# Which experts a mixture-of-experts stage starts with, how its columns are filled, and its first and last step taken out of the loop

## The chip, the cores and the metric

The kernel runs on one core of one Trainium2 chip. The metric is device time in microseconds (us), read as the median of a few runs; lower is better. Before the change the median of three runs was 944.57 us (943.24 to 945.4).

## The reference, cut to what matters

The program is one denoising step of a two-layer backbone: layer 0 mixes tokens with an RWKV-7 and a convolution branch, layer 1 with differential attention. Each layer ends in a mixture of experts (MoE), and only that part is changed. Two streams of 128 tokens of width 1024 pass through it, a prompt and a sample:

```python
def hier_moe(h, rg_w, rg_b, re_w, re_b, w_gate, w_up, w_down):
    g_idx = argmax(h @ rg_w + rg_b)                  # one of 4 groups
    e_in = (h @ re_w + re_b) of the chosen group     # 8 experts in it
    top_v, top_i = lax.top_k(e_in, 2)                # two experts for each token
    gates = one_hot(g_idx * 8 + top_i) * g_p * softmax(top_v)
    hid = silu(h @ w_gate[e]) * (h @ w_up[e])        # 1024 -> 256
    out = (hid * gates) @ w_down[e]                  # 256 -> 1024
```

With 256 tokens and two picks each there are 512 picks. The weights of one expert are 1024 x 512 (gate and up) and 256 x 1024 (down) in float32: 3 MiB.

How the picks fall for this input, by evaluating the reference's router (picks of prompt and sample together; experts that nobody picked are left out):

| layer | expert: picks |
|---|---|
| 0 | 0: 91, 1: 33, 2: 48, 3: 47, 4: 51, 5: 4, 6: 24, 7: 134, 8: 1, 9: 1, 24: 18, 25: 16, 26: 5, 27: 2, 28: 13, 29: 3, 30: 18, 31: 3 |
| 1 | 8: 67, 9: 45, 10: 157, 11: 98, 12: 15, 13: 3, 14: 69, 15: 4, 16: 2, 17: 2, 18: 3, 19: 6, 20: 5, 24: 2, 25: 4, 26: 2, 27: 4, 28: 10, 30: 8, 31: 6 |

## The kernel before

The MoE of a layer runs in steps. One step handles 128 slots: four *columns* (`NC = 4`) of 32 slots (`CH = 32`), and each column belongs to one expert. An expert with n picks needs n/32 chunks, rounded up: 28 chunks and so 7 steps in layer 0, 32 chunks and 8 steps in layer 1. Each column has one buffer for one expert's weights (`EW[:, c]`), of three parts: gate and up for the first four tiles of the width (`gu0`, 1 MiB), for the other four (`gu1`, 1 MiB), and `down` (1 MiB). A part is reloaded as soon as TensorE (PE) is through with it in the step before, and only if the column's expert changes (the flags `M_LOAD` in `meta`). SyncE (SP) issues these loads in the order gu0, gu1, down of step i, then gu0 of step i+1, and it waits before each part for PE.

One step on PE: the gate and up products (line 1282, first half on gu0, second on gu1), the *gather* of the next step's tokens by a product with a 0/1 selection matrix (L1247), two pairs of transposes (L1295, L1298), the *scatter* of the last step's result into the sums (L1258), the down product (L1310). ScalarE (ACT) and VectorE (DVE) copy results out of PSUM and form the hidden values between them; DVE also builds the selection and gate matrices of the next step.

What stands ahead of the loop. Experts of step 0 are chosen from the prompt's counts alone, while the sample's stream is still being normalised: `first_keys` and `first_ranks` rank the experts by these counts, and the four least picked (above zero) are the first step's, so that their 12 MiB of weights can be on the way. When both streams' counts are there, DVE works out the rest: chunks of the remaining experts in order of their number, cut into four equal runs, one for each column; the expert and the reload flag of each step and column go to `meta` as integers, and `sig(..., "meta")` releases SP, ACT, PE and DVE, which all read the number of steps from it. Only then does any of them enter its loop.

`warm(n)` issues n dummy products on PE where it would idle. GpSimd (POOL) waits for the second step's down product and then loads the gate rows and norm parameters that the stage after needs (L765, L756; 2 MiB).

Of the kernel before, what the change touches and what calls it, by code (L numbers as in the profile page):

```python
# [15 lines left out]
ALU = mybir.AluOpType  # L16
# [46 lines left out]
NCST = C_G4 + 64  # L63


def constants():
# [22 lines left out]
    c[:, C_M8:C_M8 + 8] = np.arange(8) - 1000.0  # L89
    return c  # L90
# [97 lines left out]
def build(nc, a, o):  # L188
# [41 lines left out]
    small = view(region(320), 320)  # L230
# [19 lines left out]
    BK2 = Banks(ps, [6], S("filled_side"), {"dve": S("drained_side")})  # L250
# [184 lines left out]
    def plan_first(l):  # L435
        for h2 in range(2):
            BK.add(("xT", f"e{l}", 0, h2), "act" if h2 == 0 else "dve")
        if l == 0:
            BK.add(("mix", 0, 1, 0), "dve")
        BK.add(("lg", l, 0), "dve")  # L440
        for kind in ("first", "ranked", "early"):
            BK.add((kind, l), "dve")
        if l == 0:
            BK.add(("mix", 0, 1, 1), "dve")

    def plan_moe(l):
# [9 lines left out]
        for kind in ("base", "eid"):  # L456
            BK2.add((kind, l), "dve")

# [149 lines left out]
    R_EID, R_F, R_RF, R_F4 = 952, 1004, 1036, 1068  # L608
    R_FLAG, R_D = R_ZERO, R_ZERO + 64
# [24 lines left out]
    def _(sp):  # L634
# [26 lines left out]
        for l in range(2):  # L661
# [17 lines left out]
            steps = sp.value_load(meta[0:1, 0, 0:1], min_val=MINS, max_val=MAXT)  # L679
            with sp.Fori(1, steps) as it:  # L680
# [9 lines left out]
                sp.wait_ge(S(f"down{l}"), it * 2 + 2)  # L690
# [21 lines left out]
    def _(pool):  # L712
# [63 lines left out]
        for l in range(2):  # L776
# [4 lines left out]
            pool.wait_ge(S(f"down{l}"), 6)  # L781
# [20 lines left out]
    def _(pe):  # L802
# [376 lines left out]
        def first_rows(l):  # L1179
# [3 lines left out]
            pe.matmul(bank[0:1, 0:NC], cst[0:32, C_COL:C_COL + 1], rt_[0:32, R_F4:R_F4 + NC], start=True, stop=True)  # L1183
            pe.matmul(bank[:, 32:64], rt_[0:32, R_NB:R_NB + P], ident[0:32, 0:32], start=True, stop=True)
            pe.matmul(bank[:, 64:96], rt_[0:32, R_ZERO:R_ZERO + P], ident[0:32, 0:32], start=True, stop=True)\
                .then_inc(filled, 1)

# [10 lines left out]
        first_rows(0)  # L1198
        project_out(0, 1, 1, range(7, KT))


        def moe(l):
# [5 lines left out]
            filled_side = S("filled_side")  # L1208
            rows(l, 0)
# [20 lines left out]
            side_free("base")  # L1230
            pe.wait_ge(S("nchunks"), l + 1)
            bank, nb = side("base"), rt_[0:32, R_NB:R_NB + P]
            pe.matmul(bank[:, 0:32], nb, SU[0:32, 0:32], start=True, stop=True)
            pe.matmul(bank[:, 32:33], nb, ones[0:32, 0:1], start=True, stop=True)
            pe.matmul(bank[0:32, 64:65], UI[0:32, 0:32], nb[:, 0:1], start=True, stop=True).then_inc(filled_side, 1)
# [6 lines left out]
            def gather(n, tiles=range(KT)):  # L1242

                pe.wait_ge(S(f"selected{l}"), n + 1)
                for k in tiles:
                    for s in range(NS):
                        mm = pe.matmul(ps[:, 4 + k // 4, (k % 4) * P:(k % 4 + 1) * P], hb[:, s, k * P:(k + 1) * P],  # L1247
                                       sel[:, s, :], start=(s == 0), stop=(s == 1))
                    if k % 4 == 3:
                        mm.then_inc(S(f"gathered{l}"), 1)  # L1250

            def scatter(n):

                pe.wait_ge(S(f"y_read{l}"), n + 2)
                pe.wait_ge(S(f"y_read_dve{l}"), n + 2)
                for s in range(NS):
                    for half in range(2):
                        mm = pe.matmul(ps[:, 2 * s + half, :], tG[:, s * P:(s + 1) * P],  # L1258
                                       ysb[:, half * 512:(half + 1) * 512], start=False, stop=False,
                                       skip_group_check=True)  # L1260
                return mm

            warm(6)
            gather(0, range(4))
            side_free("eid")
            pe.wait_ge(S("ended"), l + 1)
            pe.matmul(side("eid")[0:1, 0:NC * MAXS], ones[0:32, 0:1], rt_[0:32, R_CMP:R_CMP + NC * MAXS],
                      start=True, stop=True).then_inc(filled_side, 1)

            gather(0, range(4, KT))  # L1270
            pe.wait_ge(S("cleared"), 4 * l + 4)
            BK2.wait_drained(pe, ("eid", l))
            pe.wait_ge(S(f"meta{l}"), 1)
            steps = pe.value_load(meta[0:1, 0, 0:1], min_val=MINS, max_val=MAXT)
            with pe.Fori(0, steps) as n:
                pe.wait_ge(S(f"xg_act{l}"), n + 1)
                pe.wait_ge(S(f"xg_dve{l}"), n + 1)
                for h in range(2):
                    pe.wait_ge(S(f"gu{h}_loaded{l}"), n * 64 + 64)
                    for k in range(4 * h, 4 * h + 4):  # L1280
                        for c in range(NC):
                            mm = pe.matmul(ps[32 * c:32 * c + 32, 6, :], xg[:, k, 32 * c:32 * c + 32],  # L1282
                                           EW[:, c, k * 512:(k + 1) * 512],
                                           start=(k == 0), stop=(k == KT - 1), skip_group_check=True)
# [1331 lines left out]
```

## Time and profile before

| | us |
|---|---|
| median of 3 runs | 944.57 |
| the profiled execution | 940.24 |
| its span | 938.4 |
| PE busy in it | 845.4 |
| DVE busy in it | 493.0 |

The MoE of layer 0 is the stretch from about 422 to 568 us of the span (7 steps), that of layer 1 from about 758 to 920 us (8 steps). The remaining 2 us of the execution's time lie around the span. In the timeline a row of PE is a run of equal instructions; the trace counts two matmul records for each float32 product. "[5.57 <-DMA ...]" behind a row is the idle time of that engine just before it and what ended it.

### The profile page before, as it was taken

Reading aid. Unit: us, or ns where it says so; the run is one execution under the profiler, and the core shown is the slowest. Engines: PE = TensorE matmul, PEld = TensorE weight load, DVE = VectorE, ACT = ScalarE, POOL = GpSimd, SP = SyncE. Lnnn points to the kernel's source line nnn. Section 1 sums busy time; section 2 is a strip of 40 time slices with the busy share of each in tenths; the row PEclk is TensorE's granted clock in tenths of the full one; section 3 lists DMA queues with packets and bytes.
Section 4 is the critical chain, followed back from the end, with each engine's and each line's share of the span. In section 5 each row is a group of like instructions: output and inputs, shape, how many; then the busy total and the mean of one; then the engine's idle time right before and its main releaser. Section 6 shows DMA issues by size and latency. Waiting matters only on the chain. (4 is left out here: it accounts for less than half of the span.)

```text
span 938.4 us, 14579 instructions
## 1 busy us (share of the span) xinstructions
PE 845.4 (90%) x5328; PEld 516.2 (55%) x5328; DVE 493.0 (53%) x1287; ACT 192.3 (20%) x538; POOL 41.9 (4%) x62
## 2 busy tenths in 40 slices
PE   3899989999999989989799978999879887999893
PEld 0687865777677675573345435444555752444351
DVE  1244589898864684675224426011375771432356
ACT  0125631222211211121111101110562210111110
POOL 1000140000000000000000001000000000000000
PEclk9999999999999999999899989999999998999997
DMA  9941269565454410099989785544100699989961
GB/s 366 411 181 68 90 253 415 194 264 184 153 213 181 186 38 34 20 409 421 418 322 413 282 373 203 216 179 159 66 1 1 262 422 421 373 344 404 420 262 45
DMA packets 29071, 226.85 MB, mean 242 GB/s; under 512 B 4105, under 2 KB 4521, under 8 KB 8033
## 3 DMA queue, kind: packets, MB, share of 16 engines
q1 hardware_dynamic: 25504, 214.57, 57.1%
q0 software_dynamic: 3520, 11.66, 3.7%
q8 instruction: 29, 0.48, 0.2%
q14 instruction: 18, 0.14, 0.0%
HBM read 286.74 MB, written 2.39 MB: 308 GB/s over the span
## 5 line engine op out<-in xcount | busy, mean ns | idle before, releaser
L1282 PE MATMUL ps<-arena 128*32 128x512 f32 x960 | 114.9, 628 | 25.6 <-DMA arena<-in_w_exp 23.6
L1282 PEld LDWEIGHTS ps<-arena 128*32 128x32 f32 x960 | 31.2, 115 | 105.7 <-issue 74.1
L1467 ACT ACTIVATE arena<-ps 128x256 f32<-128x256 f32 (+1 forms) x106 | 41.7, 435 | 212.8 <-PE ps L838 133.0
L1336 PE MATMUL ps<-arena 128*128 128x512 f32 x192 | 83.0, 592 | 0.8 <-ACT arena L1475 0.6
L922 PE MATMUL ps<-arena 128*128 128x256 f32 x368 | 81.6, 380 | 1.9 <-ACT arena L1475 1.9
L922 PEld LDWEIGHTS ps<-arena 128*128 128x128 f32 x368 | 69.0, 189 | 14.5 <-ACT arena L1475 2.1
L838 PE MATMUL ps<-arena 128*128 128x128 f32 x432 | 61.4, 278 | 14.2 <-DVE arena L2532 4.7
L1247 PEld LDWEIGHTS ps<-arena 128*128 128x128 f32 x544 | 63.0, 193 | 17.8 <-issue 10.9
L1247 PE MATMUL ps<-arena 128*128 128x128 f32 x544 | 66.6, 280 | 4.4 <-DVE arena L2348 4.4
L1029 PE MATMUL ps<-arena 128*128 128x192 f32 x320 | 65.3, 351 | 3.8 <-DVE arena L2070 1.6
L838 PEld LDWEIGHTS ps<-arena 128*128 128x128 f32 x432 | 48.4, 142 | 35.2 <-issue 10.3
L2442 DVE TENSOR_SCALAR arena<-arena 128x256 f32<-128x256 f32 x15 | 4.4, 296 | 119.1 <-ACT arena L1687 118.5
L1029 PEld LDWEIGHTS ps<-arena 128*128 128x128 f32 x320 | 55.2, 201 | 19.3 <-issue 11.5
L813 PE MATMUL ps<-arena 128*32 128x512 f32 x384 | 51.1, 636 | 15.0 <-DMA arena<-in_cst 13.0
L1336 PEld LDWEIGHTS ps<-arena 128*128 128x128 f32 x192 | 36.1, 189 | 46.4 <-issue 46.4
L1310 PE MATMUL ps<-arena 128*32 128x512 f32 x480 | 54.6, 595 | 0.0
L1258 PE MATMUL ps<-arena 128*128 128x512 f32 x120 | 54.0, 592 | 0.0
L2054 DVE SCALAR_TENSOR_TENSOR arena<-arena 128x256 f32<-128x256 f32 x120 | 52.4, 482 | 0.1
L2152 DVE COPY arena<-ps 128x256 f32<-128x256 f32 x80 | 33.9, 423 | 24.5 <-PE ps L1029 24.3
L2455 DVE COPY arena<-ps 128x512 f32<-128x512 f32 x15 | 10.4, 693 | 59.4 <-PE ps L1310 59.4
L1687 ACT ACTIVATE arena<-ps 128x256 f32<-128x256 f32 x15 | 5.8, 385 | 152.5 <-PE ps L1282 152.5
L1310 PEld LDWEIGHTS ps<-arena 128*32 128x32 f32 x480 | 13.9, 109 | 38.4 <-issue 38.4
(344 smaller groups left out, 1102.8 us busy)
## 6 DMA issues: line engine op xcount, KB each, us to landing
arena<-in_w_exp SPq DMA_DIRECT2D x180, 1024.0 KB
arena<-in_mod_w SPq DMA_DIRECT2D x24, 2048.0 KB, 7.7
arena<-in_od_in_w SPq DMA_DIRECT2D x6, 2048.0 KB, 7.6
arena<-in_ev_in_w SPq DMA_DIRECT2D x5, 2048.0 KB, 29.6
arena<-in_ev_out_w SPq DMA_DIRECT2D x2, 2048.0 KB, 7.5
arena<-gate_rows POOLq DMA_DIRECT2D x8, 512.0 KB, 9.0
arena<-in_ln POOLq DMA_DIRECT2D x4, 1024.0 KB, 11.5
arena<-in_od_out_w SPq DMA_DIRECT2D x2, 2048.0 KB, 7.6
```

Source lines behind the costliest of these rows:

```text
L813: mm = pe.matmul(bank[q:q + 32, :], cond[:, k, :], w[:, k, :], start=(k < 4), stop=(k >= 4), skip_group_check=True)
L838: mm = pe.transpose(bank[:, n * P:(n + 1) * P], t, ident)
L922: mm = pe.matmul(bank[:, n * 256:n * 256 + 256], slot(("evin", i // 4))[:, k, (i % 4) * P:(i % 4 + 1) * P], hT[:, k, :], start=(k == 0), s ...
L1029: mm = pe.matmul(BK.bank(key)[:, (i % 2) * 192:(i % 2) * 192 + 192], lt[i], now[:, i, :], start=True, stop=True)
L1247: mm = pe.matmul(ps[:, 4 + k // 4, (k % 4) * P:(k % 4 + 1) * P], hb[:, s, k * P:(k + 1) * P], sel[:, s, :], start=(s == 0), stop=(s == 1))
L1258: mm = pe.matmul(ps[:, 2 * s + half, :], tG[:, s * P:(s + 1) * P], ysb[:, half * 512:(half + 1) * 512], start=False, stop=False, skip_grou ...
L1282: mm = pe.matmul(ps[32 * c:32 * c + 32, 6, :], xg[:, k, 32 * c:32 * c + 32], EW[:, c, k * 512:(k + 1) * 512], start=(k == 0), stop=(k == K ...
L1310: mm = pe.matmul(ps[32 * c:32 * c + 32, 4 + half, :], tH[:, f * P + 32 * c:f * P + 32 * c + 32], w, start=(f == 0), stop=(f == 1), skip_gr ...
L1336: mm = pe.matmul(BK.bank(key), hT[:, k, s * T:(s + 1) * T], slot(("odin", c))[:, k, :], start=(k == 0), stop=(k == KT - 1))
L1467: BK.drained_by(A(out, take(key)[:, 0:n], ACT.Copy), key)
L2054: ins = STT(out, src, w, out, ALU.mult, ALU.add)
L2152: own.inc(V.tensor_copy(new[:, pair, 0:P], src[:, :, 0:P]))
```

## The change

Four things change together.

1. **First experts.** `C_PICK` sets which ranks the four columns start with: the most picked by the prompt, the second most, the least and the second least. Two of them are therefore experts with many chunks.
2. **The plan of the columns.** A first expert keeps its column for as many further steps as it has chunks (up to the number of steps). What is left of the columns is filled with the other experts' chunks, ordered by their picks, fewest first, instead of by their number. `first_ranks` gets a second part, and there is one more side product (`tot`, then `base`).
3. **First and last step peeled.** PE, ACT and DVE run step 0 ahead of the loop, and the last step behind it. Step 0 has no scatter and no longer waits for `meta`, which DVE now writes later, behind the places of the next step. The last step has no gather and its scatter comes ahead of its transposes.
4. **Smaller.** `warm(6)` ahead of the first gather is gone, and so are two DVE memsets; the side products use PSUM bank 7 instead of 6.

By the new rule the experts of step 0 are 7, 2, 5, 8 in layer 0 (before 5, 8, 9, 27) and 14, 11, 13, 15 in layer 1 (before 13, 15, 19, 20). Step by step, the number of columns that load a new expert is then, worked out from the picks and both plans:

| layer | before | after |
|---|---|---|
| 0 | 4, 4, 2, 1, 3, 1, 4 (19) | 4, 2, 3, 2, 3, 2, 3 (19) |
| 1 | 4, 4, 2, 1, 3, 2, 3, 2 (21) | 4, 2, 1, 3, 3, 3, 2, 3 (21) |

The core of the diff:

```diff
+    c[:, C_PICK:C_PICK + 12] = [1, 1, 0, 0, -1, -2, 0, 1, 3, 2, 0, 1]
...
             sp.wait_ge(S(f"meta{l}"), 1)
-            steps = sp.value_load(meta[0:1, 0, 0:1], min_val=MINS, max_val=MAXT)
+            steps = sp.value_load(meta[0:1, 0, 1:2], min_val=MINS, max_val=MAXT)
...
                 for h in range(2):
-                    sp.wait_ge(S(f"gu{h}_done{l}"), it + 1)
+                    sp.wait_ge(S(f"gu{h}_done{l}"), it)
...
-            for h in range(2):
-                pe.sem_inc(S(f"gu{h}_done{l}"), 1)
-            pe.sem_inc(S(f"down{l}"), 2)
...
-            warm(6)
             gather(0, range(4))
+            side_free("base")
+            pe.wait_ge(S("based"), l + 1)
...
             gather(0, range(4, KT))
+            pe.wait_ge(S(f"xg_act{l}"), 1)
+            pe.wait_ge(S(f"xg_dve{l}"), 1)
+            for h in range(2):
+                pe.wait_ge(S(f"gu{h}_loaded{l}"), 64)
+                for k in range(4 * h, 4 * h + 4):
+                    gate_up(xg, k)
+            gather(1)
+            BK2.wait_drained(pe, ("eid", l))
+            pe.wait_ge(S(f"gates{l}"), 1)
+            turn(0)
+            down(0)
+            pe.wait_ge(S(f"meta{l}"), 1)
+            last = pe.value_load(meta[0:1, 0, 0:1], min_val=MINS - 1, max_val=MAXS)
+            with pe.Fori(1, last) as n:
+                gate_ups(n)
...
+            gate_ups(last)
+            scatter(last - 1)
+            turn(last)
+            down(last)
...
+            place, other = rt_[:, R_A:R_A + 4], rt_[:, R_A + 4:R_A + 8]
+            own.link(STT(col(34), col(33), sc[0:32, 48:49], col(37), ALU.min, ALU.mult))
+            own.link(TT(col(38), col(33), col(34), ALU.subtract))
+            sig(TS(rt_[0:32, R_NB:R_NB + 32], rt_[0:32, R_T:R_T + 32], col(60), col(38), ALU.is_gt, ALU.mult), "based")
...
+            own.link(TT(by_step(kept, NC), per_col(eid[:, 0:NC], 1), by_step(eid[:, NC:], NC), ALU.subtract))
+            own.link(TT(kept, kept, held, ALU.mult))
+            own.link(TT(eid[:, NC:], eid[:, NC:], kept, ALU.add))
...
+            sig(V.memset(sc[:, 62:64], 0.0), f"meta{l}")
+            gates(0, 6, place)
+            hidden(0)
+            gathered(1)
+            step_end(0)
+            out_half(0)
+            dve.wait_ge(S(f"meta{l}"), 1)
+            last = dve.value_load(meta[0:1, 0, 0:1], min_val=MINS - 1, max_val=MAXS)
```

On PE, ahead of the loop of layer 0. Before: the count and base products, `warm(6)` (L843 x6), the two halves of the first gather (L1247 x8) with the expert row between them (L1267), then the loop's gate and up products (L1282).

```order
292 L1228 MATMUL ps<-arena 128x32
293 L1233 MATMUL ps<-arena 128x32
294 L1234 MATMUL ps<-arena 128x1
295 L1235 MATMUL ps<-arena 32x1
296 L843 MATMUL ps<-arena 128x128 x6
297 L1247 MATMUL ps<-arena 128x128 x8
298 L1267 MATMUL ps<-arena 1x48
299 L1247 MATMUL ps<-arena 128x128 x8
```

The same place after the change (gather L1230, gate and up L1219, transposes L1237 and L1240, down L1250, reading `meta` L1321):

```order
291 L1282 MATMUL ps<-arena 128x32
292 L1287 MATMUL ps<-arena 128x1
293 L1288 MATMUL ps<-arena 32x32
294 L1230 MATMUL ps<-arena 128x128 x8
295 L1296 MATMUL ps<-arena 128x72
296 L1297 MATMUL ps<-arena 128x1
297 L1298 MATMUL ps<-arena 32x1
298 L1230 MATMUL ps<-arena 128x128 x8
299 L1219 MATMUL ps<-arena 32x512 x16
300 L1310 MATMUL ps<-arena 1x48
301 L1219 MATMUL ps<-arena 32x512 x16
302 L1230 MATMUL ps<-arena 128x128 x16
```

The dummy products are gone, three side products stand between the halves of the gather, and the expert row moved from ahead of the gate and up products into their middle.

On DVE, the end of what makes `meta`. Before: the expert numbers come in from PSUM (L2391), are cast to `meta` (L2392, L2394), the memset L2395 signals it, and the copy of the gathered tokens (L2357) comes behind it.

```order
561 L2391 TENSOR_SCALAR arena<-ps 1x48
562 L2392 CAST meta<-arena 1x48
563 L2393 TENSOR_TENSOR arena<-arena 1x48
564 L2394 CAST meta<-arena 1x48
565 L2395 MEMSET arena 128x2
566 L2357 COPY arena<-ps 128x512
```

After, the copy is L2407 and stands at row 574; 31 instructions for the places of the next step (L2497 to L2535) and the four that build its selection (L2395, L2398) follow, and only then the rows of `meta`, signalled by L2552, with the gates and the hidden values of step 0 behind them:

```order
605 L2395 TENSOR_SCALAR arena<-arena 128x128 x2
606 L2398 SCALAR_TENSOR_TENSOR arena<-arena 128x128 x2
607 L2540 TENSOR_TENSOR arena<-arena 1x48
608 L2541 TENSOR_SCALAR arena<-arena 1x1
609 L2542 CAST meta<-arena 1x1
610 L2543 CAST meta<-arena 1x1
611 L2544 TENSOR_SCALAR arena<-ps 1x48
612 L2546 TENSOR_TENSOR arena<-arena 1x48
615 L2549 CAST meta<-arena 1x48
617 L2551 CAST meta<-arena 1x48
618 L2552 MEMSET arena 128x2
```

So 47 instructions now stand between the copy and the signal that stood ahead of it before.

## Rows read from the trace of the kernel before

**Rows 1.** The page: engines, the transfers of SP's queue, the chain that ended last.
```profile
PE 845.4 (90%) x5328; PEld 516.2 (55%) x5328; DVE 493.0 (53%) x1287; ACT 192.3 (20%) x538; POOL 41.9 (4%) x62
q1 hardware_dynamic: 25504, 214.57, 57.1%
PE 10%; DMA 5%; SPq 2%; DVE 2%; issue 1%; DVEq 0%
```
**Rows 2.** Timeline of PE, layer 0: start us, us, what, idle before.
```profile
442.02 3.62 PE L1282 MATMUL ps<-arena 128*32 128x512 f32 x32
451.21 5.68 PE L1282 MATMUL ps<-arena 128*32 128x512 f32 x32 [5.57 <-DMA arena<-in_w_exp]
456.82 3.84 PE L1247 MATMUL ps<-arena 128*128 128x128 f32 x32
464.47 3.64 PE L1310 MATMUL ps<-arena 128*32 128x512 f32 x32
467.93 7.07 PE L1282 MATMUL ps<-arena 128*32 128x512 f32 x64
486.03 7.06 PE L1282 MATMUL ps<-arena 128*32 128x512 f32 x64
508.88 3.65 PE L1282 MATMUL ps<-arena 128*32 128x512 f32 x32 [1.13 <-DMA arena<-in_w_exp]
551.38 5.10 PE L1282 MATMUL ps<-arena 128*32 128x512 f32 x32 [6.10 <-DMA arena<-in_w_exp]
564.05 3.64 PE L1310 MATMUL ps<-arena 128*32 128x512 f32 x32
```
**Rows 3.** Timeline of PE, layer 1.
```profile
788.25 6.12 PE L1282 MATMUL ps<-arena 128*32 128x512 f32 x32 [6.29 <-DMA arena<-in_w_exp]
885.42 5.33 PE L1282 MATMUL ps<-arena 128*32 128x512 f32 x32 [2.80 <-DMA arena<-in_w_exp]
916.42 3.64 PE L1310 MATMUL ps<-arena 128*32 128x512 f32 x32
```
**Rows 4.** Windows: length, PE, PEld, DVE, ACT, POOL busy (instructions), granted clock, DMA share, GB/s.
```profile
400.00:424.00 24.00, 20.31 (x165) 17.77 (x167) 17.19 (x73) 5.81 (x15) 0.00 (x0) 0.93 1.01 421
468.00:476.00 8.00, 8.00 (x77) 2.97 (x70) 1.18 (x3) 0.39 (x1) 1.56 (x3) 1.00 0.91 340
416.00:418.00 2.00, 1.96 (x10) 1.96 (x11) 1.39 (x9) 0.00 (x0) 0.00 (x0) 0.54 1.00 418
```
**Rows 5.** Timeline, what lies ahead of the first steps.
```profile
397.92 2.11 SPq L667 DMA_DIRECT2D arena<-in_w_exp  x4
413.52 2.15 PE L843 MATMUL ps<-arena 128*128 128x128 f32 x12
416.04 2.89 PE L1247 MATMUL ps<-arena 128*128 128x128 f32 x16 [0.37 <-DVE arena L2348]
419.94 0.06 DVE L2395 MEMSET arena<- 128x2 f32 x1
421.19 0.69 DVE L2357 COPY arena<-ps 128x512 f32<-128x512 f32 x1 [1.19 <-PE ps L1247]
752.59 2.05 PE L1247 MATMUL ps<-arena 128*128 128x128 f32 x16 [0.85 <-DVE arena L2348]
756.90 0.69 DVE L2357 COPY arena<-ps 128x512 f32<-128x512 f32 x1 [1.19 <-PE ps L1247]
```
**Rows 6.** Timeline of DVE, layer 0: instructions like those that are added.
```profile
421.80 0.22 DVE L2398 TENSOR_SCALAR arena<-arena 128x3 f32<-128x3 f32 x1
421.92 0.15 DVE L2399 TENSOR_SCALAR arena<-arena 128x1 f32<-128x1 f32 x1
422.44 0.23 DVE L2402 SCALAR_TENSOR_TENSOR arena<-arena 128x64 f32<-128x64 f32 x1
422.70 0.23 DVE L2403 SCALAR_TENSOR_TENSOR arena<-arena 128x64 f32<-128x64 f32 x1
```
**Rows 7.** SP's own queue, instructions of one line: duration ns, first and last start.
```profile
L683 SPq FUSED_REGOPS  x65: 56/147/147, 422.1 to 884.4; - x65
```

More of the change, by code:

```diff
@@ L440, in plan_first @@
         BK.add(("lg", l, 0), "dve")
-        for kind in ("first", "ranked", "early"):
+        for kind in ("first", "ranked", "early", "frows"):
             BK.add((kind, l), "dve")
@@ L1209, in moe, with scatter @@
+            def scatter(n):
+                for s in range(NS):
+                    for half in range(2):
+                        mm = pe.matmul(ps[:, 2 * s + half, :], tG[:, s * P:(s + 1) * P],
+                                       ysb[:, half * 512:(half + 1) * 512], start=False, stop=False,
+                                       skip_group_check=True)
+                mm.then_inc(S(f"scattered{l}"), 1)
             rows(l, 0)
@@ L1236, in moe @@
-            for h in range(2):
-                pe.sem_inc(S(f"gu{h}_done{l}"), 1)
-            pe.sem_inc(S(f"down{l}"), 2)
+            pe.matmul(side("tot")[:, 0:1], ones[0:32, :], sc[0:32, 33:34], start=True, stop=True)
+            pe.matmul(side("tot")[0:32, 32:64], rt_[0:32, R_NB:R_NB + 32], ident[0:32, 0:32], start=True, stop=True)\
+                .then_inc(filled_side, 1)
             BK.wait_drained(pe, ("hb", l, 1, 1))
             BK.wait_drained(pe, ("pos", l))
[L1242 to L1261, printed above, removed]
-            warm(6)
@@ new lines, in moe @@
+            inside, slot = rv(R_T4, 64, "p (s n) -> p s n", s=NS), rv(R_ZERO, 64, "p (s n) -> p s n", s=NS)
+            pos = take(("pos", l))[:, 0:64].rearrange("p (s n) -> p s n", s=NS)
+            own.inc(STT(inside, pos, float(CH), both(rv(R_F, 32)), ALU.is_lt, ALU.mult))
+            own.inc(STT(slot, pos, 1.0, both(rv(R_RF, 32)), ALU.add, ALU.add))
+            read(STT(later, both(rv(R_F, 32)), -float(CH), pos, ALU.mult, ALU.add), "pos")
+            own.wait()
+            own.link(TT(slot, slot, inside, ALU.mult))
@@ new lines, in moe @@
+            own.link(TT(beyond, beyond, both(delta), ALU.mult))
+            own.link(TT(later, moved, beyond, ALU.add))
+            own.inc(TT(rv(R_T, 64), P1, rv(R_SL, 64), ALU.mult))
+            own.link(TT(rv(R_T4, 64), P2, rv(R_SL, 64), ALU.mult))
+            for pick, v in enumerate((R_T, R_T4)):
+                own.inc(V.tensor_reduce(sc[:, 42 + 2 * pick:44 + 2 * pick], rv(v, 64, "p (s n) -> p s n", s=NS), AX, ALU.add))
+            own.wait()
+            at, chunk, column, lin = sc[:, 42:46], sc[:, 6:10], sc[:, 10:14], rv(R_LIN, 4)
@@ L2457, in sum_half @@
+            with dve.Fori(1, last) as n:
+                hidden(n)
+                gathered(n + 1)
+                step_end(n)
+                out_half(n)
+            hidden(last)
+            out_half(last)
             def sum_half(s, half):
```

379 lines of the change are left out of this document (219 added, 160 removed).

## Prediction

> **What bounds the kernel now.** I read the page first: PE is busy 90% of the span and the chain that ended last is PE with 5% of DMA in it [rows 1]. That share of DMA is all in the loads of expert weights, so the question is what the two MoE stages wait for, and the timelines of PE over them answer it. A step without a wait takes 18.10 us (gate and up products begin at 467.93 and again at 486.03) [rows 2]: 7.05 for gate and up, 11.05 for gather, transposes, scatter and down product. Steps with 3 or 4 new experts wait in the middle, for gu1: 5.57, 1.13 and 6.10 us in layer 0 [rows 2], 6.29 and 2.80 us in layer 1 [rows 3]. Behind the long ones the second half takes 5.1 to 6.1 us instead of 3.65, because the clock has fallen to the lower level. So five waits cost 21.9 us and their slow halves 1.5 to 2.5 us each.
>
> The transfers run at 421 GB/s while loads are queued [rows 4], 2.49 us for 1 MiB and 7.47 us for an expert. Two new experts in a step cost 14.9 us, less than a step of PE; three 22.4 and four 29.9, more than a step. Latency, from the first loads: issued at 397.92 [rows 5], 20 MiB later (12 of step 0, 8 of gu0 and gu1 of step 1) PE goes on at 451.21 [rows 2]; 53.3 less 49.8 leaves 3.5 us, which I split into 1.65 before bytes flow and 1.85 behind the last. SP adds 0.8 where it waited for PE: half of the step from 486.03 ends at 489.6, 6 MiB take 14.9, and PE goes on at 508.88, 4.4 later.
>
> **Loads and order.** The change doesn't save a load: 19 and 21 before and after, by the table of steps. It evens them out. Before, the dear steps are 1, 4 and 6 of layer 0 (4, 3, 4 experts). After, layer 0 alternates 2 and 3 and its mean over steps 1 to 6 is 18.7 us of transfers for 18.1 of PE: almost balanced. Layer 1 gets 3, 3, 3, 2, 3 at its end, and the three in a row are bound by transfers, 22.4 us a step.
>
> **The later `meta`.** Before, the signal comes at 420.0 [rows 5] and no load is late by it: SP's next loads wait for PE anyway, which begins step 0 behind the copy at 421.19, and the 12 MiB of step 0 flow until 429.4 (397.92 + 1.65 + 29.9). After, 47 DVE instructions stand between the copy of the gathered tokens and the signal. One that waits for its predecessor costs up to 0.26 us from start to start, one that doesn't 0.12 [rows 6]: 5.6 to 12.2 us for the 47. From which of them wait I take 9.1, and 0.6 for the copy. The copy itself begins at 421.19 [rows 5]; 0.6 is added for the two more side products between the halves of the gather and for the later output tile of `mix` (PE now waits for `early_columns`). Behind the signal SP reads `meta` twice more: before, the last register group begins at 422.1 [rows 7], 2.1 behind the memset at 419.94 [rows 5], and lasts some 1.4, so 3.5 us, and 1.65 until bytes flow.
>
> **The clock at the front.** In layer 0 the clock was low at 416 to 418 [rows 4] although six dummy products ran from 413.52, and the first half of the gather took 2.89 instead of 2.05 us [rows 5]. After, PE has nothing from 413.9 to 416.2; both halves and the side products then fall into the slow stretch. Bounds: 0, and 2.7, if all of the first half (2.05) and of the side products (some 0.6) runs at half speed; I take 2.0 in layer 0. In layer 1 the same half ran at 2.05 us [rows 5] with the dummies; without them I take 1.0, midway.
>
> So bytes flow again at 421.19 + 0.6 + 2.0 + 9.7 + 3.5 + 1.65 = 438.6 us in layer 0, and at 756.90 + 0.6 + 1.0 + 9.7 + 5.15 = 773.35 in layer 1. The transfers stand still for 9.2 and about 7 us. That hole is the price of the change, and step 0 on PE hides it only as long as step 1 needs two experts.
>
> **Step 0 on PE.** The scatter of step 0 (3.5 us) is gone, but DVE now makes gates and hidden values behind `meta`; the reciprocal and its neighbours take some 4.5 us behind the signal, so the down product of step 0 begins about when it did (438.6). It costs nothing, since gate and up of step 1 must wait for loads until 438.6 + 5.0 + 1.85 = 445.4 anyway.
>
> **Layer 0 to its end.** From 438.6 on the queue never runs dry but once. Up to gu1 of the last step 15 experts less one down part of three are loaded: 42 MiB, 104.6 us. POOL's 2 MiB fall among them: before, 468 to 476 moved only 340 GB/s [rows 4], and I count 5.0 us. Once the issue of down (step 5) comes late, 1.4. Then 1.85, the second half 3.5, and the rest of the last step. That rest is 11.05 less the gather's 3.67 (3.84 in the row, 3.67 from start to start) [rows 2] plus 1.1 for the hidden values and the copy that the gather used to cover: 8.5. The last wait for gu1 is 2.4 us; 2.80 us dropped the clock [rows 3], 1.13 did not [rows 2]: bounds 0 and 1.9, I take 0.95. The sum: 438.6 + 104.6 + 5.0 + 1.4 + 1.85 + 3.5 + 8.5 + 0.95 = 564.4, against 564.05 + 3.64 = 567.7 before [rows 2]: 3.3 us earlier.
>
> **Layer 1 to its end.** Let S be 773.35. Gate and up of step 1 end at S + 15.3, step 1 at S + 26.4. Step 2 loads one expert, so the queue is dry until its down part and POOL's loads come at S + 28.7. From there 9 MiB to gu1 of step 3 (S + 51.1), 18 MiB to gu1 of step 5 (S + 95.9), gate and up of step 5 over at S + 101.3. Step 5's rest, step 6 and the loads of step 7, which can't be issued before: gu1 of step 7 lands at S + 136.5, end at S + 148.5. Two waits of 2.4 to 3.7 us on this path, 0.95 each: S + 150.4 = 923.75, against 916.42 + 3.64 = 920.1 [rows 3]: 3.7 us later.
>
> **The sum.** -3.3 + 3.7 = +0.4. The same arithmetic put to the kernel before ends its layers 0.5 and 1.3 us too early; half of that belongs to the new path as well, +0.9. So +1.3 us, 941.5 for an execution like the profiled one (940.24) and 945.9 against the median of 944.57.
>
> The Trainium skill ("DMA: Bandwidth & Descriptors", on where 436 GB/s comes from) says that the HBM side binds at about 358 GB/s. By it 1 MiB would take 2.93 us, every step with two experts would wait too, transfers alone would set both layers, and the hole behind `meta` would be a loss of some 7 to 9 us each. The 421 GB/s measured here speak against it.
>
> **Rivals.**
> - *The front keeps its clock and short waits don't drop it.* For it: in layer 1 no clock fell in a stretch like that of layer 0; 1.13 us cost nothing. Against it: 416 to 418. It gives 3.0 at the fronts and 2.85 at the three waits: 945.9 - 5.9 = 940.0.
> - *Slower: the hole behind `meta`, full.* Place: between the signal and the first bytes of step 1. Both layers are bound by loads behind it, so each microsecond of it counts once per layer; and low clock in layer 1 too (+1.0) and at all three waits (+2.85) makes 949.8. It decides as soon as waits of 2.4 us drop the clock, or DVE's 47 instructions take over 9.5 us.
> - *Even loads hide all transfers.* Then the waits (21.9) and most slow halves go, and 5 us of the two gathers: 912. For it stands only the mean of 18.7 against 18.1; against it the 3, 3, 3 and the hole.
> - *The plan does something else* on the chip (ties, or a router's pick that rounds otherwise), so that a load more or less falls in. One load is 7.5 us where transfers bind; about 938 or 953.
>
> **How the numbers follow.** Forecast 0.45, first rival 0.25, slower 0.22, hidden 0.03, another plan 0.05. A change within 0.2% (1.9 us) can't be told from none here. The forecast's own range is 943 to 948.5: 0.26 of it within, 0.13 slower, 0.06 faster. First rival: faster 0.22, same 0.03. Together faster 0.33, same 0.31, slower 0.36. For 8 in 10 the range takes in the first and the slower rival: 939.5 to 951.5.
>
> **What would show it.** Right: the signal of `meta` about 9.7 us behind the copy; a hole of 7 to 9 us in the DMA windows of each layer before step 1; gate and up of step 1 waiting for loads near 445 instead of 451 us; unbroken 421 GB/s in layer 0 from there; waits at every step of three experts in layer 1 from step 3 on; layer 0 some 3 us shorter and layer 1 some 4 longer; 7 and 8 steps and 40 expert loads as before. Wrong: a hole under 4 us, no wait in layer 1's run of threes, or a layer's end off by more than 4 us from 564 and 920.5 (923.75 less what layer 0 gained).

## The result, and the profile after

The changed kernel takes 950.38 us (median of 11 runs, 944.35 to 954.47) against 943.47 us (11 runs, 941.46 to 945.95) for the kernel before on the same chip: a ratio of 1.0065, 95% interval 1.0039 to 1.009. It is 0.65% slower. The forecast was 945.9 us, 0.14% above the median it was set against. The range of 8 in 10 (939.5 to 951.5) held the time, near its upper end; the forecast's own range (943 to 948.5) didn't. The slower rival (949.8), which adds nothing to the forecast but more low clock, came nearest.

The profiled execution after has a span of 950.1 us, before 938.4. The page of the changed kernel, beside [rows 1]: engines, SP's transfers, the chain that ended last.

```profile
PE 842.4 (89%) x5228; PEld 510.5 (54%) x5228; DVE 491.4 (52%) x1329; ACT 190.7 (20%) x536; POOL 41.9 (4%) x62
q1 hardware_dynamic: 25504, 214.58, 56.4%
DMA 8%; PE 7%; DVE 2%; SPq 2%; issue 1%; ACT 0%; DVEq 0%
```

PE has 3 us less to do, and the bytes are the same. In the chain DMA has gone from 5% to 8% and PE from 10% to 7%: the end is now set more by loads. Where they come late is seen in PE's timeline over layer 0 (start us, us, what, idle before and its releaser), beside [rows 2] and the PE rows of [rows 5]:

```profile
407.99 1.95 PE L1160 MATMUL ps<-arena 128*128 128x36 f32 x16 [0.23 <-issue]
...
418.74 3.76 PE L1230 MATMUL ps<-arena 128*128 128x128 f32 x16 [2.35 <-DVE arena L2398]
...
423.55 3.79 PE L1230 MATMUL ps<-arena 128*128 128x128 f32 x16
428.17 3.65 PE L1219 MATMUL ps<-arena 128*32 128x512 f32 x32 [0.83 <-issue]
...
442.12 0.44 PE L1240 MATMUL ps<-arena 128*128 128x128 f32 x2 [2.40 <-DVE arena L2427]
443.24 3.64 PE L1250 MATMUL ps<-arena 128*32 128x512 f32 x32 [0.68 <-ACT arena L1727]
448.55 3.65 PE L1219 MATMUL ps<-arena 128*32 128x512 f32 x32 [1.68 <-DMA arena<-in_w_exp]
454.73 5.34 PE L1219 MATMUL ps<-arena 128*32 128x512 f32 x32 [2.53 <-DMA arena<-in_w_exp]
...
492.99 8.62 PE L1219 MATMUL ps<-arena 128*32 128x512 f32 x64 [2.80 <-DMA arena<-in_w_exp]
...
517.85 3.65 PE L1219 MATMUL ps<-arena 128*32 128x512 f32 x32 [1.58 <-DMA arena<-in_w_exp]
...
557.51 5.29 PE L1219 MATMUL ps<-arena 128*32 128x512 f32 x32 [3.27 <-DMA arena<-in_w_exp]
```

The two long waits of before (5.57 and 6.10) have become many short ones, and behind those of 2.53 us and more the half takes 5.3 us instead of 3.65 (at 492.99 both halves stand in one row, 8.62 instead of 7.06). The same in layer 1, beside [rows 3]:

```profile
783.29 3.65 PE L1219 MATMUL ps<-arena 128*32 128x512 f32 x32 [1.79 <-DMA arena<-in_w_exp]
789.51 5.34 PE L1219 MATMUL ps<-arena 128*32 128x512 f32 x32 [2.57 <-DMA arena<-in_w_exp]
...
832.68 5.34 PE L1219 MATMUL ps<-arena 128*32 128x512 f32 x32 [3.81 <-DMA arena<-in_w_exp]
...
855.05 3.65 PE L1219 MATMUL ps<-arena 128*32 128x512 f32 x32 [2.37 <-DMA arena<-in_w_exp]
...
877.42 5.34 PE L1219 MATMUL ps<-arena 128*32 128x512 f32 x32 [3.81 <-DMA arena<-in_w_exp]
...
918.20 5.34 PE L1219 MATMUL ps<-arena 128*32 128x512 f32 x32 [2.69 <-DMA arena<-in_w_exp]
```

DVE and SP's queue at the front of layer 0, beside [rows 5] and [rows 7]: the copy of the gathered tokens, the `meta` signal, SP's first issue behind it.

```profile
427.38 0.69 DVE L2407 COPY arena<-ps 128x512 f32<-128x512 f32 x1 [2.28 <-PE ps L1230]
...
436.60 0.06 DVE L2552 MEMSET arena<- 128x2 f32 x1
```
```profile
440.50 3.66 SPq L669 DMA_DIRECT2D arena<-in_w_exp  x8
```

And windows, beside [rows 4] (length, busy time of PE, PEld, DVE, ACT, POOL with instructions, granted clock, DMA share, GB/s):

```profile
416.00:428.00 12.00, 8.99 (x42) 8.34 (x42) 6.30 (x34) 2.75 (x5) 0.00 (x0) 0.57 1.02 423
432.00:442.00 10.00, 7.71 (x66) 4.70 (x66) 9.06 (x39) 0.98 (x2) 0.00 (x0) 1.00 0.01 6
472.00:474.00 2.00, 2.00 (x24) 0.61 (x20) 0.05 (x1) 0.00 (x0) 1.42 (x3) 1.00 0.83 225
770.00:776.00 6.00, 4.33 (x38) 3.85 (x34) 5.54 (x20) 0.98 (x2) 0.00 (x0) 1.00 0.04 16
800.00:806.00 6.00, 6.00 (x42) 1.93 (x44) 1.98 (x8) 0.98 (x2) 0.00 (x0) 1.00 0.01 4
```

432 to 442 is the hole: 10 us with 6 GB/s. At 416 to 428, which takes in nearly all of the gather, the clock is 0.57, close to the 1.2 GHz level.

**Where the 11.7 us of the two profiled spans lie.** The stages are cut at L1160 (before L1158), the router's product that opens the front of a MoE stage, and at the product that follows the last down product (L1358 after).

| stretch | before | after | difference |
|---|---|---|---|
| start to the router product of layer 0 | 404.84 | 407.99 | +3.15 |
| front of layer 0, to the first gate product | 17.29 | 20.18 | +2.9 |
| steps of layer 0 | 145.5 | 142.75 | -2.75 |
| steps of layer 0 to router product of layer 1 | 173.8 | 174.2 | +0.4 |
| front of layer 1 | 16.45 | 17.70 | +1.25 |
| steps of layer 1 | 162.2 | 168.85 | +6.65 |

Not all of the first 3.15 us is the change's. The router products of the prompt (first row before, second after) and the new product of `first_columns`:

```profile
385.26 1.87 PE L1158 MATMUL ps<-arena 128*128 128x36 f32 x16
```
```profile
387.74 1.87 PE L1160 MATMUL ps<-arena 128*128 128x36 f32 x16
398.61 0.40 PE L1192 MATMUL ps<-arena 32*128 32x64 f32 x2 [0.97 <-DVE arena L2344]
```

Up to the prompt's router product 2.5 us are lost in code that is the same; 340 to 360 us shows a clock of 0.77 after and 0.93 before. The other 0.7 us lies between the two router products of the layer, where `first_columns` is new and waits for DVE; in layer 1 the same stretch grows by 0.5 (part of the +0.4 in the table). Without the 2.5 us the pair differs by 9.2 us, against 6.9 for the medians. In the steps of both layers (all terms measured from start to start, so a wait counts 0.1 us or more above its row), the removed scatter of step 0 and gather of the last step save 4 x 3.6 = 14.4 us. Waits for weights grow from 24.2 to 32.4 (+8.2), slow halves from 7.8 to 11.9 (+4.1), and waits for DVE and ACT, in step 0 mostly (442.12 and 443.24 above), from 3.2 to 8.4 (+5.2). That makes +3.1 of the +3.9; 0.8 us are small gaps.

### The profile page after: what moved, and what is told of

Its sections match the earlier page's. It is cut to its first block and busy times, and to the rows that moved or that the text cites. A ratio compares the mean times of both kernels' runs of the same rounds, so it can differ in the third digit from the quotient of the medians.

```text
span 950.1 us, 14296 instructions
## 1 busy us (share of the span) xinstructions
PE 842.4 (89%) x5228; PEld 510.5 (54%) x5228; DVE 491.4 (52%) x1329; ACT 190.7 (20%) x536; POOL 41.9 (4%) x62
## 3 DMA queue, kind: packets, MB, share of 16 engines
q1 hardware_dynamic: 25504, 214.58, 56.4%
## 5 line engine op out<-in xcount | busy, mean ns | idle before, releaser
L1219 PE MATMUL ps<-arena 128*32 128x512 f32 x960 | 119.9, 647 | 31.7 <-DMA arena<-in_w_exp 30.0
L1219 PEld LDWEIGHTS ps<-arena 128*32 128x32 f32 x960 | 31.7, 117 | 115.1 <-issue 70.9
L1375 PE MATMUL ps<-arena 128*128 128x512 f32 x192 | 83.0, 592 | 0.8 <-ACT arena L1515 0.6
L924 PEld LDWEIGHTS ps<-arena 128*128 128x128 f32 x368 | 69.0, 189 | 14.5 <-ACT arena L1515 2.1
L840 PE MATMUL ps<-arena 128*128 128x128 f32 x432 | 62.5, 281 | 14.2 <-DVE arena L2649 4.7
L840 PEld LDWEIGHTS ps<-arena 128*128 128x128 f32 x432 | 49.5, 144 | 35.7 <-issue 10.7
L1230 PEld LDWEIGHTS ps<-arena 128*128 128x128 f32 x480 | 59.6, 205 | 16.0 <-issue 16.0
L1230 PE MATMUL ps<-arena 128*128 128x128 f32 x480 | 62.9, 292 | 4.6 <-DVE arena L2398 4.6
L1031 PE MATMUL ps<-arena 128*128 128x192 f32 x320 | 63.3, 344 | 3.0 <-DVE arena L2116 1.1
L815 PE MATMUL ps<-arena 128*32 128x512 f32 x384 | 51.1, 636 | 15.1 <-DMA arena<-in_cst 12.9
L1031 PEld LDWEIGHTS ps<-arena 128*128 128x128 f32 x320 | 53.6, 196 | 18.5 <-issue 10.6
L1375 PEld LDWEIGHTS ps<-arena 128*128 128x128 f32 x192 | 36.1, 189 | 46.4 <-issue 46.4
L1250 PE MATMUL ps<-arena 128*32 128x512 f32 x480 | 54.6, 595 | 3.0 <-ACT arena L1727 2.3
L1258 PE MATMUL ps<-arena 128*128 128x512 f32 x104 | 47.0, 594 | 0.0
L1250 PEld LDWEIGHTS ps<-arena 128*32 128x32 f32 x480 | 14.5, 109 | 38.8 <-issue 37.4
```

Source lines behind the costliest of these rows:

```text
L815: mm = pe.matmul(bank[q:q + 32, :], cond[:, k, :], w[:, k, :], start=(k < 4), stop=(k >= 4), skip_group_check=True)
L840: mm = pe.transpose(bank[:, n * P:(n + 1) * P], t, ident)
L924: mm = pe.matmul(bank[:, n * 256:n * 256 + 256], slot(("evin", i // 4))[:, k, (i % 4) * P:(i % 4 + 1) * P], hT[:, k, :], start=(k == 0), s ...
L1031: mm = pe.matmul(BK.bank(key)[:, (i % 2) * 192:(i % 2) * 192 + 192], lt[i], now[:, i, :], start=True, stop=True)
L1219: mm = pe.matmul(ps[32 * c:32 * c + 32, 6, :], xs[:, k, 32 * c:32 * c + 32], EW[:, c, k * 512:(k + 1) * 512], start=(k == 0), stop=(k == K ...
L1250: mm = pe.matmul(ps[32 * c:32 * c + 32, 4 + half, :], tH[:, f * P + 32 * c:f * P + 32 * c + 32], w, start=(f == 0), stop=(f == 1), skip_gr ...
```

## The experiments

All start from the changed kernel. Ratios are to the kernel before on the same chip, with 95% intervals; kernels of one group ran on one chip. "Layers" are the steps of layer 0 and layer 1 in the profiled execution (before 145.5 and 162.2, changed 142.8 and 168.9). The times expected in the first group were set against 943.5 us for the kernel before; on that chip it took 938.89, so only the ratios can be held against them.

### What the parts cost (first group)

**The dummy products back at the front.** Ahead of the first gather:

```diff
+            for _ in range(6):
+                pe.matmul(ps[:, 6, 0:P], ident, ident, start=True, stop=True)
             gather(0, range(4))
```

> The changed kernel with six dummy products on PE (on PSUM bank 6) put back ahead of the first half of the first gather. Theory 'hole' (the time is set by the stretch without transfers between the 12 MiB of step 0 and the loads of step 1, and each us of it counts once per layer): the dummies pull the copy of the gathered tokens ahead by what the clock gives back, 3.4 us at most in layer 0 and 1.4 in layer 1 (the gather's halves took 3.76, 3.79 and 3.45, 2.05 us against 2.05 at full clock), so 1 to 4 us off 950.4: 946 to 949. Rival 'plan' (three steps of three experts in a row in layer 1 cost the time, whenever they start): no change, 949.5 to 951. Rival 'front clock' as the whole loss: 943.5.

Measured: 943.79 us against 938.89, ratio 1.0047 [1.0021, 1.0073]; layers 142.7 and 164.7. The timeline of PE in this kernel, the gather of both layers:

```profile
420.39 3.75 PE L1230 MATMUL ps<-arena 128*128 128x128 f32 x16 [0.54 <-DVE arena L2400]
...
757.45 2.02 PE L1230 MATMUL ps<-arena 128*128 128x128 f32 x16 [0.75 <-DVE arena L2400]
```

In layer 1 the dummies keep the clock and the front is 16.26 us instead of 17.70; in layer 0 the gather stays at 3.75 us and the front at 20.18. The dummies themselves took 1.88 us there and 1.60 in layer 1: in layer 0 the clock was low already when they ran. This execution alone would say that the dummies do nothing for layer 0; the later kernels with dummies say otherwise (third group). The gain, 0.2 to 0.5% (the changed kernel stood at 1.0065 and 1.0098), isn't separated from nothing by the intervals; 946 to 949 had been expected, a ratio of 1.003 to 1.006.

**`meta` early.** The product for `eid` goes ahead of gate and up, and DVE writes `meta` right behind the copies of the gathered tokens, with the places of the next step behind it:

```diff
-    R_B1, R_D, R_FLAG = R_ZERO, R_ZERO + 32, R_SL
+    R_B1, R_D, R_FLAG = R_ZERO, R_ZERO + 32, R_CMP - NC
...
+            own.inc(TT(by_step(held, NC), step_no(1), per_col(BS[0:1, 64:68], 1), ALU.is_lt))
...
+            own.link(V.tensor_copy(meta[0:1, 0, M_LOAD + NC:M_LOAD + NC * MAXT], flag[:, NC:]))
+            sig(V.memset(sc[:, 62:64], 0.0), f"meta{l}")
```

> The changed kernel with the rows of meta made straight behind the copy of the gathered tokens, ahead of the 35 instructions for the places of step 1, and the expert row on PE ahead of gate and up of step 0. Theory 'hole': the signal comes 6.5 us earlier in each layer (427.98 + 2.1 instead of 436.6 in layer 0), the stretch without transfers shrinks from 10 to about 4 us and from 7 to about 1, gather of step 1 is 1 to 2 us later without cost, each layer ends about 6 us earlier: 938 (936 to 941), below the kernel before. Rival 'plan': the runs of three bind from step 3 in layer 1 whatever the start; only layer 0 gains: 944 to 947. Rival 'front clock': no change beyond 1 us, 950.

Measured: 936.82 us against 938.89, ratio 0.9979 [0.996, 0.9998]; layers 136.2 and 162.4. Timeline of DVE and a window of this kernel:

```profile
422.21 0.69 DVE L2406 COPY arena<-ps 128x512 f32<-128x512 f32 x1 [0.55 <-PE ps L1230]
424.73 0.06 DVE L2510 MEMSET arena<- 128x2 f32 x1
```
```profile
428.00:430.00 2.00, 2.00 (x20) 0.47 (x12) 1.69 (x12) 0.00 (x0) 0.00 (x0) 1.00 0.09 37
430.00:440.00 10.00, 6.53 (x60) 4.83 (x60) 9.42 (x30) 1.65 (x4) 0.00 (x0) 1.00 0.97 383
```

The signal comes 2.5 us behind the copy instead of 9.2. Of the hole some 2.5 us are left (37 GB/s at 428 to 430), and 430 to 440 moves 383 GB/s. The two layers together are 12.9 us shorter than in the changed kernel, and the ratio falls by 0.9 to 1.2% (0.3 to 0.8% below the kernel before had been expected, it is 0.2%). The place of this one block of DVE's work, with the product that it reads, turns a loss into a small gain. Four halves are still slow, behind waits of 2.76 to 3.82 us.

**POOL's loads put into the hole.**

```diff
-            pool.wait_ge(S(f"down{l}"), 4)
+            pool.wait_ge(S(f"gu0_done{l}"), 1)
```

> The changed kernel with POOL's 2 MiB (gate rows and norm parameters) issued behind the first half of gate and up of step 0 instead of behind the down product of step 1, so that they fall into the stretch without transfers. Theory 'hole' with transfers binding behind it: 5 us less of queue in layer 0, and the waits of 1.07 and 3.81 us at step 3 of layer 1 shrink by about 5: 941 to 943. Rival 'plan': layer 0 the same, layer 1 not, 945 to 946. Rival 'front clock': 950.

Measured: 942.29 us, ratio 1.003 [1.0011, 1.0049]; layers 139.6 and 160.2. The signal comes no earlier, but 2 MiB of transfers that fell among the experts' loads now use the hole, and the kernel regains 0.35 to 0.7% of the 0.65 to 1.0% that it had lost. That is less than the theory of the hole had expected (below the kernel before) and about what its rival 'plan' had, though that rival's reason, no gain in layer 1, is wrong. The Trainium skill ("DMA: Bandwidth & Descriptors", on issuing engines not being separate DMA queues) says that transfers interleave on the same 16 engines whichever engine issued them. The runs agree: the layers become 3.2 and 8.6 us shorter by nothing but the time at which POOL's bytes flow. In layer 1 that is more than the 5 us the bytes take, and there one half is slow instead of four.

**The gather back in the last step.**

```diff
             gate_ups(last)
+            gather(last + 1)
             scatter(last - 1)
```

> The changed kernel with the gather put back into the last step (its result is not used). My step 'the last step gives 2.6 us per layer': gather 3.7 more, hidden values covered again: 5 us slower in all, 955 to 956. Rival (peeling the last step gives nothing, since hidden values and down part are waited for anyway): within 1 us of 950.4.

Measured: 954.8 us, ratio 1.0156 [1.0126, 1.0186]; layers 148.5 and 167.6. Against the changed kernel's 1.0065 and 1.0098 that is 0.6 to 0.9%, 5.5 to 8.5 us for two gathers (the interval touches that of the second measurement of the changed kernel). The forecast's 2.6 us a layer holds or is a little low. In the profiled pair layer 0 is 5.7 us longer and layer 1 1.2 us shorter, so one execution doesn't place it.

### Plan and signal apart (second group)

**The old order of experts, `meta` late**, and in the second kernel **the old order with `meta` early**:

```diff
-    c[:, C_PICK:C_PICK + 12] = [1, 1, 0, 0, -1, -2, 0, 1, 3, 2, 0, 1]
+    c[:, C_PICK:C_PICK + 12] = [0, 0, 0, 0, 0, 1, 2, 3, 0, 1, 2, 3]
...
-            own.inc(STT(col(60), bank[0:32, 0:1], float(CH), cst[0:32, C_COL:C_COL + 1], ALU.mult, ALU.add))
+            own.inc(STT(col(60), bank[0:32, 0:1], 0.0, cst[0:32, C_COL:C_COL + 1], ALU.mult, ALU.add))
```

> The changed kernel with the plan of before alone: the four least picked first, the other experts in order of their number, so 4, 4, 2, 1, 3, 1, 4 and 4, 4, 2, 1, 3, 2, 3, 2 loads a step; the order of the work on every engine is the changed one. Theory 'hole with an even plan as its cover': four experts (20 us of gate and up) now start behind the stretch without transfers, so step 1 waits 8 to 10 us longer than in the changed kernel and its 3, 2, 3 later on come cheaper: 7 us slower than the changed kernel, 1.3 to 1.5% above the kernel before. Rival 'the new plan is what costs': faster than the changed kernel, 0 to 0.3% below the kernel before, since the last steps' gathers are gone.

> Early meta with the plan of before: the other corner of the square of plan and place of meta. Theory: the late meta costs the plan of before more (four experts behind the hole) than the new one: e5 less e8 is 10 to 13 us, against 8 us for the new plan; e8 itself stands within 0.3% of the kernel before, since a stretch of some 4 us without transfers is left and each last step saves 2.6 us. Rival: both plans lose the same 8 us to the late meta.

Measured: late 956.41 us against 942.47, ratio 1.0149 [1.0122, 1.0177], layers 151.8 and 164.4; early 941.45 us, ratio 1.0003 [0.9976, 1.0029], layers 145.1 and 157.4. The timeline of PE in the late one, layer 0:

```profile
454.32 6.39 PE L1219 MATMUL ps<-arena 128*32 128x512 f32 x32 [5.96 <-DMA arena<-in_w_exp]
...
465.54 5.91 PE L1219 MATMUL ps<-arena 128*32 128x512 f32 x32 [4.83 <-DMA arena<-in_w_exp]
...
566.99 6.38 PE L1219 MATMUL ps<-arena 128*32 128x512 f32 x32 [7.34 <-DMA arena<-in_w_exp]
```

With four new experts in step 1 the hole stands in two waits of 5.96 and 4.83 us. That fills the square:

| ratio to before | `meta` late | `meta` early |
|---|---|---|
| old order | 1.0149 | 1.0003 |
| new order | 1.0065, again 1.0098 | 0.9979 |

The late signal costs 1.46% (about 14 us) with the old order and 0.9 to 1.2% with the new; the new order saves 0.5 to 0.8% where the signal is late. Where it is early it saves 0.24%, which the intervals don't tell from nothing.

**Another order of picks, `meta` early.** First experts and gaps so that the loads of the steps become 4, 2, 3, 2, 2, 3, 2 in layer 0 (one load fewer) and 4, 2, 2, 2, 4, 2, 2, 3 in layer 1:

```diff
-    c[:, C_PICK:C_PICK + 12] = [1, 1, 0, 0, -1, -2, 0, 1, 3, 2, 0, 1]
+    c[:, C_PICK:C_PICK + 12] = [1, 0, 0, 1, -1, 0, 1, -2, 3, 0, 1, 2]
```

> The kernel with early meta and another choice of first experts: most, least, second least, second most picked, columns in this order. By both plans worked out: 4, 2, 3, 2, 2, 3, 2 (18 loads) and 4, 2, 2, 2, 4, 2, 2, 3 (21). Theory 'loads in their order, one by one, against 18.1 us of PE' (the arithmetic of the prediction): 2 us less in layer 0 and 4 less in layer 1 than e2, so 1.5 less than 0.21% below before becomes 0.7 to 0.9% below the kernel before (931 where before takes 938.9). Rival (only the hole counts, the plan behind it does not): as e2, 0.1 to 0.3% below.

Measured: 928.52 us against 942.47, ratio 0.9871 [0.9841, 0.9902]; layers 133.9 and 156.0. It beats both kernels, by more than the 0.7 to 0.9% expected. In layer 1 of this kernel:

```profile
835.48 5.04 PE L1219 MATMUL ps<-arena 128*32 128x512 f32 x32 [6.28 <-DMA arena<-in_w_exp]
...
894.36 3.65 PE L1219 MATMUL ps<-arena 128*32 128x512 f32 x32 [2.59 <-DMA arena<-in_w_exp]
```

There is one wait of 6.28 us, at the step with four new experts, and the half behind it is slow (5.04 us). The kernel to compare is the one with `meta` early and the new order, whose layer 1 has two waits of 3.8 us and one of 2.76 with slow halves: there gate and up wait 23.1 us for weights over both layers and layer 1 takes 162.4, here 18.0 and 156.0 (the changed kernel waits 30.0). In layer 1 the number of loads is the same, so one dear step among steps of two was cheaper than three steps of three in a row. In layer 0, 2.3 us shorter, there is also one load fewer.

**`meta` early and the dummies.** The edits of the first two experiments together.

> Early meta and the six dummies together. Theory 'hole': with early meta the loads of step 1 are at hand sooner, so what the clock gives at the front still counts: 1 to 2 us less than e2, 0.3 to 0.4% below the kernel before. Rival (fronts overlap, PE waits at step 1 anyway): as e2, 0.2% below.

Measured: 934.61 us against 942.47, ratio 0.9926 [0.9897, 0.9955]; layers 137.9 and 160.2. It is lower than with `meta` early alone (0.9979), and further below the kernel before than the 0.3 to 0.4% expected, but on another chip, and layer 0 was longer; see the next group.

### The slow halves (third group)

**The best order with the dummies**, and **the same with POOL's loads later in layer 0**:

```diff
-            pool.wait_ge(S(f"down{l}"), 4)
+            pool.wait_ge(S(f"down{l}"), 8 - 4 * l)
```

> Early meta, the other choice of first experts (e6) and the six dummies. Theory: what the dummies gave in e7 against e2 (0.5%, intervals of 0.3% each) comes on top, since with two experts in each early step PE and not the loads sets most steps: 1.6 to 1.8% below the kernel before. Rival (the gain in e7 was scatter: in e1 layer 0's front was not shorter): as e6, 1.2 to 1.4% below.

> e9 with POOL's 2 MiB of layer 0 issued behind step 3 instead of step 1, ahead of two steps with two experts each; layer 1 as it was. Theory (loads are served in the order of issue, and 5 us of POOL's fall on a step with three experts): the waits of 3.05 and 0.89 + 1.33 us at steps 2 and 3 of layer 0 fall to about 1 us, 3 to 4 us off with the slow half: 0.3 to 0.4% below e9. Rival: no change, the waits move to steps 4 and 5.

Measured: 927.39 us against 941.78, ratio 0.9865 [0.9821, 0.9909], layers 135.0 and 155.2; with POOL later 929.79 us, 0.9883 [0.9838, 0.9928], layers 137.4 and 156.5. The dummies add nothing to the time that can be told from the other order alone (0.9871), so what they seemed to give in the group before isn't established. Moving POOL's 2 MiB gained nothing. The waits of step 3 went, and longer ones stand at step 5, before it and in its middle:

```profile
524.58 3.65 PE L1219 MATMUL ps<-arena 128*32 128x512 f32 x32 [3.16 <-DMA arena<-in_w_exp]
532.03 5.34 PE L1219 MATMUL ps<-arena 128*32 128x512 f32 x32 [3.81 <-DMA arena<-in_w_exp]
```

So the 2 MiB came cheaper in the hole, where the transfers stood still, and not at this later place.

At the front of layer 0 the dummies do show. The first half of the gather in this kernel:

```profile
420.67 2.02 PE L1230 MATMUL ps<-arena 128*128 128x128 f32 x16 [0.81 <-DVE arena L2399]
```

In the four kernels with dummies it took 3.75 us (the first experiment), 3.05, 2.28 and 2.02, and the front 20.18, 17.29, 16.81 and 16.26. In the eight experiments and controls without them and in the changed kernel it took 3.75 or 3.76 every time, and the front 18.2 to 20.2.

**The changed kernel once more**, as a control.

> The changed kernel itself, as a fixed point beside the others on this chip. 0.65% above the kernel before (0.4 to 0.9).

Measured: 952.0 us against 941.78, ratio 1.0098 [1.0064, 1.0132]; layers 142.1 and 169.3. Its waits and slow halves stand where those of the first profile stood, within 1 us. The ratio is a little above the range expected (0.4 to 0.9%); the intervals of the two measurements overlap.

**PE kept busy in the waits.** Between the halves of gate and up, from step 1 on:

```diff
+                    if h == 1:
+                        pe.wait_ge(S(f"y_read{l}"), n)
+                        for _ in range(8):
+                            pe.matmul(ps[:, 4, 0:P], ident, ident, start=True, stop=True)
```

> The changed kernel with eight dummy products between the two halves of gate and up in every step but the first (1.1 us of PE that fall into the wait where there is one). The changed kernel's profile shows seven slow halves of 5.3 us instead of 3.65, behind waits of 2.5 to 3.8 us. Theory 'the slow halves are part of the loss': waits of 2.5 us become 1.4, which never dropped the clock, those of 3.8 become 2.7, which still may; three or four slow halves go that were on the path, 1.7 each, for 1.1 in the two steps without a wait: 3 to 4 us less, 0.2 to 0.3% above the kernel before. Rival (the halves are absorbed by the next wait): 0 to 2 us more, 0.7 to 0.9% above.

Measured: 946.23 us against 941.78, ratio 1.0054 [1.0025, 1.0082]; layers 143.2 and 165.1. Timeline of PE in this kernel, a step of layer 1 (the eight products stand as 16 instructions):

```profile
868.84 2.05 PE L1328 MATMUL ps<-arena 128*128 128x128 f32 x16
872.73 3.65 PE L1219 MATMUL ps<-arena 128*32 128x512 f32 x32 [1.84 <-DMA arena<-in_w_exp]
```

Where the changed kernel waited 3.81 us and then took 5.34, this one computes dummies for 2.05 us, waits 1.84 and takes 3.65. No half of any step with the dummies is slow. The time falls by 0.44% by the ratios (4.1 us; 5.8 by the medians of that chip), though the intervals of the two touch; in 76 of the 84 pairs of their runs this kernel is the faster. The result lies between the two expectations, and the eight products took 2.05 us where 1.1 had been expected. Layer 1 gains 4.2 us against the control. Layer 0 loses 1, as its dummies run in steps without a wait too. Part of the gain may be chance: the front of layer 0, which the edit doesn't touch, took 18.17 us in this profile and 20.17 in the control. So the slow halves are worth some 4 us, less what the dummies cost and with that doubt. This can't be added to what the early signal gives back: that experiment recovered the whole loss with four slow halves left.

## Why the prediction was near, and where it fell short

The range held the time, but the change was forecast at 1.3 us and measured at 6.9. The direction came out right from chances that were nearly even over faster, same and slower (0.33, 0.31, 0.36), so it says little. The mechanism of the hole came out nearly to the microsecond; what was missing is the low clock behind short waits.

**The signal and the hole: confirmed.** Copy to signal was 9.2 us (forecast 9.7), signal to SP's first issue 3.9 (3.5), and transfers are busy again at about 442.3, 14.9 behind the copy (14.85). Less the 2.5 us lost in unchanged code that is 439.8 against 438.6. In layer 1 they flow again at about 776.9, also 14.9 behind the copy; less the 3.2 us by which the prompt's router product of layer 1 came later that is 773.7 against 773.35. That the late signal is the price of the change was shown by moving its block, with both orders of experts.

**The clock at the fronts: sized a little low.** Behind the sample's router product the copy came 3.0 us later in layer 0 and 1.4 in layer 1, and 0.7 and 0.5 us more were lost ahead of it at `first_columns`: 3.7 and 1.9 against 2.6 and 1.6. I laid the clock on the missing dummies. They explain layer 1. In layer 0 they kept it in part or wholly in three of four kernels and not in the first experiment, so there they are one cause, and what lowers the clock ahead of them stays open.

**Step 0 on PE: as said.** The removed scatter gave nothing: PE waits for DVE and ACT instead, and for weights behind that, at 448.55.

**Layer 0 to its end: the step that failed first.** From the bytes to the end it took 128.7 us, not 125.8. I had steps that transfers set and PE follows, one wait of 2.4 us with half a slow half. There were five waits, three of 2.5 to 3.3 us, each with a full slow half of 1.6 to 1.7 us. "From 438.6 on the queue never runs dry but once" was wrong too: 472 to 474 moved 225 GB/s. Of the 2.9 us, 2.4 fall before the last gu1 is there (113.4 us from the first bytes, forecast 111.0 with POOL's loads and the late issue), 0.5 behind it. A slow half delays the release of its buffers, and in a stage where PE and transfers are nearly balanced (18.1 and 18.7 us a step) a delay of either is passed on to the other. That last sentence is argued from the rows; no run isolates it.

**Layer 1 to its end: the same term.** 154.8 us, not 150.4. The waits stand where they were forecast, at every step of three from step 3 on, with the dry stretch of step 2 (800 to 806). Two halves at 0.95 us each were charged; four cost 1.7 us each. From the second half of step 3 to that of step 5 it took 44.7 us (832.68 to 877.42), the 44.8 that the loads alone take, so the slow half of step 3 is covered. Those of steps 1 (behind 2.57 us, not forecast at all), 5 and 7 stand on the path: 5.1 us where 1.9 were charged. Dummies in the waits took 4.2 us back in this layer.

**The term that was mis-sized**, then, is the low clock behind short waits: 2.85 us for three halves in the sum, where seven slow halves came to 11.9 and removing them was worth about 4 us of the time. The bounds had been 0 and 1.9 us for each; the measured value lies near the upper one. The slower rival named it ("as soon as waits of 2.4 us drop the clock"). The wait of 2.37 us didn't, but the forecast's waits came out at 2.5 to 3.8, and those did.

**The gain of the last step: borne out** at 2.6 us a layer or a little more, by putting the gather back.

**The other rivals.** SP's queue moved 214.58 MB against 214.57, so no load was added or saved (an expert is 3.15 MB, and the kernel with one load fewer moved 211.43), and the waits stand at the steps that the table of loads gives. The even loads hid nothing: 30.0 us of waits in gate and up against 23.6. The prediction counted 21.9 of these; it left out two short ones in layer 1 (0.64 and 1.02).

The Trainium skill ("DMA: Bandwidth & Descriptors", on where 436 GB/s comes from) would have had the HBM side bind at about 358 GB/s. The changed kernel moved 423 GB/s at 416 to 428, so that rule doesn't hold here, with one core running, and the loss isn't from there. Nor would all have followed that the prediction drew from it: at that rate the 6 MiB of two experts take 17.6 us by estimate, still less than a step's 18.10.

## What to carry to other kernels

When a plan is made better at the price of making it later, compute first when the transfers that hang on it run out. Here 7 us of small DVE instructions between the data and the signal cost 0.9 to 1.5%, more than the even plan gave, and writing the signal first cost nothing that shows in the time. In a stage where PE and transfers are nearly balanced, count the waits of 2.5 to 4 us at their length plus 1.7 us wherever PE and not the loads sets what follows; a few dummy products between the halves kept the clock here, at a price of 2 us in each step that had no wait.

## What the runs showed that was not expected

- Whether a short wait lowers the clock isn't a matter of its length alone. Behind two waits of 3.20 us, one with `meta` early alone and one with `meta` early and the dummies:

```profile
466.44 5.34 PE L1219 MATMUL ps<-arena 128*32 128x512 f32 x32 [3.20 <-DMA arena<-in_w_exp]
```
```profile
464.77 3.65 PE L1219 MATMUL ps<-arena 128*32 128x512 f32 x32 [3.20 <-DMA arena<-in_w_exp]
```

  In all profiles together the shortest wait for weights with a slow half behind it is 2.10 us (old order, `meta` early), and the longest without one 3.20. Behind 3.27 us and more every half took 5.0 to 6.6 us.
- The same code ahead of the MoE took 2.5 us longer in one profile than in the other, with a granted clock of 0.77 against 0.93 at 340 to 360. The first gate product of layer 0 came at 422.44 in one experiment and at 429.66 in another. Cut a profile into stages before comparing spans: what lies ahead of the change is not its doing.
- From the `meta` signal to SP's first issue it took 3.9 us (436.60 to 440.50), and to the first bytes about 5.7. In layer 1 it was the same 3.9 and 5.7. A signal that decides what is loaded has to come that much before the queue runs dry.
